# Feed-forward down weights: sums by accumulating DMA a round ahead, and a re-ordered VectorE queue

## What is computed

```python
def conv_ffn(h, w_up, conv_w, conv_b, w_down):      # h = rmsnorm(x)
    u = h @ w_up                                    # 512 x 5632
    gate, up = u[..., :D_FF], u[..., D_FF:]         # D_FF = 2816
    gp = jnp.pad(gate, ((0, 0), (CONV_W - 1, 0), (0, 0)))
    conv = conv_b + conv_w[0] * gp[:, 0:S]
    for i in range(1, CONV_W):
        conv = conv + conv_w[i] * gp[:, i:i + S]
    return (jax.nn.silu(conv) * up) @ w_down        # x = x + this
```

## Time and profile before

| | us |
|---|---|
| median of 3 runs | 1114.54 |
| lowest and highest | 1112.5, 1115.76 |
| profiled execution: time | 1112.34 |
| profiled execution: span | 1110.5 |
| PE busy | 1078.2 |
| DVE busy | 765.6 |
| ACT busy | 490.3 |
| POOL busy | 158.5 |

### The profile page before, as it was taken

The page is one execution under the profiler, slowest core; times in us unless marked ns, Lnnn a source line. Parts: engine busy times, 40 slices in busy tenths (PEclk is TensorE's granted clock), DMA queues, the critical chain, the costliest instruction groups (busy, mean ns, idle before and its releaser), DMA issues.

```text
span 1110.5 us, 15662 instructions
## 1 busy us (share of the span) xinstructions
PE 1078.2 (97%) x5896; PEld 919.9 (83%) x5896; DVE 765.6 (69%) x1061; ACT 490.3 (44%) x755; POOL 158.5 (14%) x126
## 2 busy tenths in 40 slices
PE   6999999999999999989999999999999999999986
PEld 5888778888999888879788888878888999888886
DVE  4588666676986565998343656866676986565986
ACT  6366554443433334445652245444443433434442
POOL 6100030112000112012020221030112000112012
PEclk9999999999999999999999999999999999999998
DMA  6512032225242224241222211132225242224232
GB/s 193 157 59 74 22 112 95 94 94 169 88 146 100 95 95 154 73 141 64 76 77 95 81 52 58 59 112 95 94 94 171 86 155 92 95 94 155 72 117 88
DMA packets 39704, 112.38 MB, mean 101 GB/s; under 512 B 4769, under 2 KB 9537, under 8 KB 39650
## 3 DMA queue, kind: packets, MB, share of 16 engines
q1 hardware_dynamic: 34592, 106.45, 28.2%
q0 software_dynamic: 1152, 2.88, 1.6%
q10 hardware_dynamic: 3906, 2.31, 1.1%
HBM read 108.21 MB, written 2.88 MB: 100 GB/s over the span
## 4 chain that ended last, share of the span: by engine, by line
PE 43%; DVE 6%; ACT 2%; issue 1%; DMA 1%; POOL 0%; DVEq 0%; ACTq 0%; POOLq 0%
PE PS L444 33%; PE PS L497 6%; DVE WL L1260 1%; DVE DL_Z L1348 1%; PE PS L744 1%; ACT WH L863 1%; DVE DL_W L1348 1%; DVE X L1789 0%; PE PS L776 0%; PE PS L763 0%; DVE X L1393 0%; ACT SQ L893 0%; PE PS L747 0%; DVE DRAW_Z L1385 0%; DMA RAW<-w_down 0%
## 5 line engine op out<-in xcount | busy, mean ns | idle before, releaser
L444 PE MATMUL PS<-XH,WH 128*128 128x512 f32 x992 | 394.3, 397 | 8.7 <-DVE XL L1277 8.6
L444 PE MATMUL PS<-XH,WL 128*128 128x512 f32 x992 | 387.4, 391 | 0.0
L444 PE MATMUL PS<-XL,WH 128*128 128x512 f32 x992 | 387.1, 390 | 0.0
L444 PEld LDWEIGHTS PS<-XH,WH 128*128 128x128 f32 x992 | 186.9, 188 | 52.5 <-issue 11.4
L1260 DVE TENSOR_TENSOR WL<-WRAW,WH 128x1024 fp32r<-128x1024 f32 x137 | 193.4, 1412 | 51.5 <-ACT WH L863 50.8
L444 PEld LDWEIGHTS PS<-XL,WH 128*128 128x128 f32 x992 | 187.1, 189 | 39.2 <-issue 1.7
L444 PEld LDWEIGHTS PS<-XH,WL 128*128 128x128 f32 x992 | 186.8, 188 | 39.3
L863 ACT CAST WH<-WRAW 128x1024 fp32r<-128x1024 f32 x137 | 142.4, 1043 | 156.3 <-DMA WRAW<-w_up 99.5
L1834 POOL TENSOR_TENSOR CV<-CV,R 128x512 f32<-128x512 f32 x40 | 62.1, 1553 | 498.7 <-ACT CV L909 498.7
L497 PE MATMUL PS<-AH,DH_Z 128*128 128x256 f32 x352 | 99.5, 283 | 7.9 <-DVE X L1393 7.3
L1294 DVE TENSOR_TENSOR GS<-PS,R 128x512 f32<-128x512 f32 x44 | 30.4, 692 | 110.7 <-PE PS L444 110.5
(11 more groups left out here) (219 smaller groups left out, 1515.1 us busy)
## 6 DMA issues: line engine op xcount, KB each, us to landing
WRAW<-w_up SPq DMA_DIRECT2D x88, 512.0 KB, 3.2
WRAW<-w_bin SPq DMA_DIRECT2D x24, 512.0 KB, 3.2
DRAW_W<-w_down SPq DMA_DIRECT2D x24, 384.0 KB, 3.7
DRAW_W<-w_down SPq DMA_DIRECT2D x24, 320.0 KB, 3.4
WRAW<-w_qkv SPq DMA_DIRECT2D x11, 512.0 KB, 4.5
RAW<-w_down SPq DMA_DIRECT2D x12, 384.0 KB, 3.0
RAW<-w_down SPq DMA_DIRECT2D x12, 320.0 KB, 2.9
WRAW<-w_o SPq DMA_DIRECT2D x7, 512.0 KB, 3.2
```

Of the source, the lines that this page charges most:

```text
L444: last = mm(PS[:, bank], w[:, c:c + P], x[:, kb], start=start and n == 0 and w is wh and x is hi, stop=stop and n == len(kbs) - 1 and w is wl)
```

## The change

- The sums Z1 and Z3 of all rounds are made by DMA: SP loads W21 into one of four buffers WSUM0 to WSUM3 (which lie over RW and GS, free in the down phase), and POOL's accumulating DMA adds W22 or W11. `sum_z1` and `sum_z3` are gone from DVE. The loads for rounds n+1 and n+2 are issued at the start of the phase, those for n+3 in round n+1.
- The 40 multiplications of silu by R on POOL and 4 on DVE are gone; `values` on DVE multiplies the value half from PSUM by R into RW (44 times), and `gated` multiplies the silu onto it. PE's up units wait for `value_ready` where they waited for `gated_ready`.
- The low parts of X (`x_lo`) move from rounds n+1 to n+3 all into round n+3.
- Around the start of the down phase and in all rounds, low parts, sums and takes change places in DVE's queue; ACT's follow at the start. The zeroing of GS's first columns is done for each chunk.

The core of the diff:

```diff
-        RAW21 = place("RAW21", [P, PAIRS[0] * P], at=place_at[0] - 32 * TH)
-        RAW22 = place("RAW22", [P, PAIRS[0] * P], at=place_at[0] - 20 * TH)
+        sums_at = place_at[0] - 32 * TH
         GS = place("GS", [P, 2, T + 2])
+        WSUM = [place(f"WSUM{i}", [P, PAIRS[0] * P], at=sums_at + 4 * i * PAIRS[0] * P) for i in range(4)]
+        assert sums_at + 16 * PAIRS[0] * P <= place_at[0]
...
+        def with_sum(n, name):
+
+            if n % 4 == 0:
+                return DRAW["Z1"] if name == "Z1" else Z3RAW
+            return WSUM[((3, 1) if name == "Z1" else (0, 2))[n % 2 == 0]]
 
...
+            def load_21(n, name):
+
+                sp.dma_start(with_sum(n, name)[:, 0:down_cols(n)], quarter(n, "W21"))\
+                    .then_inc(first_half[name, n % 2], 16)
 
...
                 sp.wait_ge(unit_done, u0 + last)
                 load_down(n, "W22")
-                sp.wait_ge(t_ready, FT * layer + F0[chunk] + 2 * PAIRS[chunk])
-                load_21(n + 1)
+                sp.wait_ge(conv_ready, FT * layer + F0[chunk] + 2 * PAIRS[chunk])
+                load_21(n + 1, "Z1")
                 sp.wait_ge(al_ready, AL_LAYER * layer + AL_COUNT[chunk] + 2 * PAIRS[chunk] + 1)
-                load_22(n + 1)
+                load_21(n + 1, "Z3")
+                load_21(n + 2, "Z1")
+                load_21(n + 2, "Z3")
 
             def load_round(n, src, next_unit):
 
                 r = n % 4
-                if r in (1, 2):
+                if r == 1:
+                    sp.wait_ge(down_lo["Z1"], n + 1)
+                    load_21(n + 2, "Z1")
                     sp.wait_ge(down_lo["Z3"], n + 1)
-                    load_22(n + 1)
+                    load_21(n + 2, "Z3")
                 if r:
                     sp.wait_ge(down_done, COUNT[n - 1, "W22"])
                     load_down(n, "W22")
...
                     load_down(n + 1, "W11")
                     sp.wait_ge(down_done, COUNT[n, "W12"])
                     load_down(n + 1, "W12")
-                if r < 2:
-                    sp.wait_ge(summed["Z3"], later(n + 1))
-                    load_21(n + 2)
...
+            def values(layer, m, par):
+
+                dve.wait_ge(unit_done, UP[layer] + 2 * m + 2)
+                tt(RW[:, 3 * par:3 * par + 2], halves(PS[:, 2 * par + 1]), halves(R[:]), ALU.mult)\
+                    .then_inc(value_ready, 1)
+
             def gated(layer, m, par):
 
-                u = UP[layer] + 2 * m
-                dve.wait_ge(unit_done, u + 2)
-                dve.wait_ge(slr_ready, FT * layer + m + 1)
-                halves = lambda t: t.rearrange("p (h t) -> p h t", h=2)
-                tt(RW[:, 3 * par:3 * par + 2], halves(PS[:, 2 * par + 1]), halves(CV[:, par]), ALU.mult)                    .then_inc(gated_ready, 1)
+                dve.wait_ge(value_ready, FT * layer + m + 1)
+                dve.wait_ge(silu_ready, FT * layer + m + 1)
+                rows = RW[:, 3 * par:3 * par + 2]
+                tt(rows, rows, halves(CV[:, par]), ALU.mult).then_inc(gated_ready, 1)
                 dve.wait_ge(gated_ready, FT * layer + m + 1)
...
                 odd_step(pairs - 2)
+                sum_z2(n)
+                weight_lo(n, "Z1")
                 evacuate_gate(layer, f, 0)
                 lo_unit(u0 + 4 * pairs - 1)
                 odd_sums(layer, chunk, f - 1, kb - 1)
                 convolve(layer, f, 0)
                 odd_lo(layer, chunk, kb - 1)
-                sum_z2(n)
-                weight_lo(n, "Z1")
+                values(layer, f, 0)
                 weight_lo(n, "W11")
                 evacuate_gate(layer, f + 1, 1)
                 even_sums(layer, f)
-                sum_z4(n)
                 convolve(layer, f + 1, 1)
                 even_lo(layer, chunk, kb)
+                sum_z4(n)
                 weight_lo(n, "W12")
+                values(layer, f + 1, 1)
+                odd_sums(layer, chunk, f + 1, kb)
+                last_lo(layer, chunk, kb, 2, 4)
+                take_w11(n)
+                last_lo(layer, chunk, kb, 4, 7)
                 weight_lo(n, "Z2")
-                dve.wait_ge(silu_ready, FT * layer + f + 2)
-                tt(CV[:, 1], CV[:, 1], R[:], ALU.mult).then_inc(slr_ready, 1)
-                odd_sums(layer, chunk, f + 1, kb)
-                last_lo(layer, chunk, kb)
 
             def down_rounds(n, st, next_unit):
 
                 take_z1(n)
-                take_w11(n)
                 weight_lo(n, "Z4")
                 weight_lo(n, "Z3")
                 take_w12(n)
-                sum_z1(n + 1)
                 take_z2(n)
-                sum_z3(n + 1)
                 sum_z2(n + 1)
                 weight_lo(n + 1, "Z1")
                 take_z4(n)
+                weight_lo(n, "W22")
+                weight_lo(n + 1, "W11")
                 sum_z4(n + 1)
-                weight_lo(n + 1, "W11")
-                weight_lo(n, "W22")
                 for m in (n + 1, n + 2):
                     take_z3(m - 1)
                     weight_lo(m, "W12")
+                    weight_lo(m, "Z2")
+                    take_z1(m)
+                    weight_lo(m, "Z4")
+                    take_w22(m - 1)
                     weight_lo(m, "Z3")
-                    take_z1(m)
-                    weight_lo(m, "Z2")
-                    take_w22(m - 1)
-                    weight_lo(m, "Z4")
-                    if st is not None:
-                        x_lo(st, 2 * (m - 1 - n))
-                    sum_z1(m + 1)
                     take_w11(m)
-                    if st is not None:
-                        x_lo(st, 2 * (m - 1 - n) + 1)
                     take_w12(m)
                     weight_lo(m, "W22")
-                    sum_z3(m + 1)
                     take_z2(m)
                     sum_z2(m + 1)
...
                 weight_lo(m, "Z2")
                 take_w11(m)
                 weight_lo(m, "Z4")
+                take_w22(m - 1)
                 weight_lo(m, "W12")
-                take_w22(m - 1)
                 weight_lo(m, "Z3")
                 if st is not None:
-                    x_lo(st, 4)
+                    x_lo(st, 0)
                 take_z1(m)
                 if st is not None:
-                    x_lo(st, 5)
+                    x_lo(st, 1)
+                    x_lo(st, 2)
                 take_z2(m)
                 weight_lo(m, "W22")
+                if st is not None:
+                    x_lo(st, 3)
                 take_z4(m)
                 if next_unit is not None:
                     lo_unit(next_unit)
+                if st is not None:
+                    x_lo(st, 4)
                 take_z3(m)
+                if st is not None:
+                    x_lo(st, 5)
                 if next_unit is not None:
                     lo_unit(next_unit + 1)
...
-                def gate(m, j):
-                    pool.wait_ge(silu_ready, m + (FT * layer + 1))
-                    nc.gpsimd.tensor_tensor(CV[:, j], CV[:, j], R[:], ALU.mult).then_inc(slr_ready, 1)
-                    pool.wait_ge(slr_ready, m + (FT * layer + 1))
-
-                def add_quarter(n, name, onto, src):
-                    pool.wait_ge(plain[name], 16 * (n // 4 + 1))
+                def add_quarter(n, name):
+                    onto, src = with_sum(n, name), "W22" if name == "Z1" else "W11"
+                    pool.wait_ge(first_half[name, n % 2], 16 * (n // 2 + 1))
                     pool.dma_start(onto[:, 0:down_cols(n)], quarter(n, src), accum_op=ALU.add)\
-                        .then_inc(added[name], 16)
+                        .then_inc(added[name, n % 2], 16)
 
                 for chunk in range(2):
-                    f0, n = F0[chunk], 4 * (2 * layer + chunk)
-                    with pool.Fori(0, 2 * PAIRS[chunk] - 2, 2) as i:
-                        for j in range(2):
-                            gate(i + (f0 + j), j)
-                    add_quarter(n, "Z1", DRAW["Z1"], "W22")
-                    add_quarter(n, "Z3", Z3RAW, "W11")
-                    gate(f0 + 2 * PAIRS[chunk] - 2, 0)
+                    n = 4 * (2 * layer + chunk)
+                    for m in range(n, n + 3):
+                        add_quarter(m, "Z1")
+                        add_quarter(m, "Z3")
                     if chunk:
-                        for m in range(6):
+                        sum_square(st + 1, 0)
+                    add_quarter(n + 3, "Z1")
+                    if chunk:
+                        sum_square(st + 1, 1)
+                    add_quarter(n + 3, "Z3")
+                    if chunk:
+                        for m in range(2, 6):
                             sum_square(st + 1, m)
```

More of the change, by code:

```diff
@@ L264, in trunk @@
         t_ready, nt2_ready, gated_ready = sem("t_ready"), sem("nt2_ready"), sem("gated_ready")
[L265 to L268 removed]
+        plain = {name: sem(f"plain_{name}") for name in ("W11", "W12", "W22")}
```

(4 more changed lines are left out.)

86 lines of the change are left out of this document (34 added, 52 removed).

## The result

The changed kernel takes 1132.03 us (median of 4 runs, 1131.35 to 1133.58) beside 1113.92 us for the kernel before on the same chip (4 runs, 1112.5 to 1115.76): a ratio of 1.0164, 95% interval 1.0144 to 1.0183. It is slower by 18 us. The forecast was slower by 3.6 us, and the range ended at 1123.

The account below looks back on a forecast made before the run. PE, busy 97% of the span, was taken as the bound, with gaps only in the down phases; -9.1+7.6+3.0+1.7+0.4 = +3.6 us on 1114.54 gave 1118.1 us, range 1104 to 1123.

Parts of the forecast that it names:

- Part 2: Down phases: W11(n+1), issued behind three loads, lands late and holds DVE at `sum_z2`, delaying PE's W22(n): +7.6 us (3.2 to 11.6).
- part 3: Round n+1: W22's load goes behind Z3's load for n+3, so PE's Z3 waits: +3.0 us (0 to 5).
- Part 1: D1 and D3: late gaps behind long `sum_z1` and x_lo go, with D1's clock loss: -9.1 us.
- Part 4: Last round of D1: six x_lo in place of two delay PE's last product and the next gate product: +1.7 us (0 to 3).
- Part 5: Start of the phase: Z2(n) also needs its own low part behind the last AL: +0.4 us (0 to 1).
- the late bound of 7.9: D0: latest forecast landing of W11(n+1), 306.3, with the burst at 298.38.
- the forecast's own part for plain loads: W11(n+1)'s landing in D0 before the 1 us taken for accumulating DMAs; landing with it was put at 305.3, burst at 298.38.
- my late end: W11(n+1): Z3's accumulation halves its load rate while both flow, by round-robin between queues; 4 us more in the sum.
- The clock: Rival: in D1 and D3 half clock follows PE's longer waits at Z1(n+1), 2x1.7 us more, 1121.5 us; chance 0.10 for both.
- Part 6: Up phases: 44 added `values` passes of 0.69 us cost nothing under DVE's waiting; without that cover some 25 us.
- W11 in time: Rival: W11(n+1) lands as fast as DVE asks, W22(n) starts earlier, part 2 becomes -6.1: 1104.4 us, chance 0.25.

Follow-up runs that it names:

- The direct measurement: Kernel before with four unneeded 0.69 us multiplications on VectorE ahead of the low part of Z1(n+1) in each down phase: 1126.7 us, 1.0109.
- the experiment: For Part 4: changed kernel with x_lo two per round as before, 1132.31 us. For Part 6: kernel before with `values` multiplication by R alone moved, 1115.91 us.
- the one with the loads in order: Changed kernel with the two orders, W11 and W12 loaded before AL's wait, DVE's start order nearly restored, POOL's second sum earlier: 1111.38 us; without additions 1104.51.
- the two orders: Changed kernel with W21's loads for n+2 behind W11, W12 (1127.56 us); with those for n+3 behind W22, W11, W12 (1123.28); both together 1114.94.

## Why the prediction was wrong

Three steps failed. Part 2 had the landing of W11(n+1) too early in D0 and D2 (11.4 us for 7.6), part 3 had the landing of W22(n+1) as if no additions ran beside it (7.5 us for 3.0), and the half clock stood at nothing (some 5.5 us that belong to no other part). With parts 1, 4 and 5 as measured, -9.0+11.4+7.5+1.4+1.7+5.5 is 18.5 of the 20.2 us between the two spans. Nearly all of the waits, with their places and releasers, were as predicted.

**Part 1, stalls that go: right.** The late starts at Z2(n+1) and Z2(n+2) are gone, 7.0 us, and D1's half clock of the earlier trace rows with them, about 2: 9 us for the 9.1 of the sum. One count in it is off: the 16 steps of a round, 9 of 0.74 and 7 of 0.33, are 9.0 us and not 8.2, which still fits into the 11.9.

**Part 2, W11(n+1) late: right in mechanism and place, in size in D1 and D3 alone.** The wait was predicted for `sum_z2(n+1)` with DRAW_W as releaser, and it is there. The landing in D1 was put 11.8 us behind the phase's start and came at 11.9. The accumulations' share was put at 1 us (0 to 2.1) and measured 0.8 to 1.65. The late starts at Z1(n+1) and W22(n) grew by 7.9 us in all, where 7.6 was the term, but that they agree so well is luck. In D1 and D3 PE's W22(n), the product for which the part was worked out, starts 1.9 us later behind the phase's start than before, as forecast (1.8). In D0 and D2 it starts 4.7 and 4.0 us later, where the term was 2.0 (0.9 to 3.0). The half clock has only 0.9 and 0.2 us of this: DVE ends the take of Z3(n), for which that product waits, at 313.30 in D0, 19.8 us behind the phase's start, where PE had started the product at 15.9 before, and in D2 it is the same 3.8 us.

```profile
312.89 0.41 DVE L1384 TENSOR_TENSOR X<-X,PS 128x256 f32<-128x256 f32 x1
```

The late starts do not show it, since PE ran Z1(n+1) at half clock while DVE caught up. By W22(n)'s start part 2 is 11.4 us. What was mis-sized is the landing with 384 KB: W11 landed 8.8 and 8.6 us behind the burst's start in D0 and D2, and not 6.9, later than the late bound of 7.9; and without additions still 7.5 and 6.9, where the forecast's own part for plain loads was 5.9. By the Trainium skill (DMA: Bandwidth & Descriptors, SWDGE vs HWDGE vs iDMA), each DMA engine takes turns between software and hardware queues, from which I had drawn my late end. The trace does not decide it: the additions make W11 0.8 to 1.65 us later, between my two ends of 0 and 2.1.

**Part 3, W22(n+1): the term that was mis-sized.** It was +3.0 (0 to 5). The late starts at Z3(n+1) are 7.5 us: 2.50, 2.61 and 2.44 in D1, D2 and D3. The issue was right, S+4.3 for S+4.0, but the landing was taken from the earlier trace rows, 3.4 us, a row of a queue without additions. It took 4.8, and the low part began 9.9 us behind S and not 8.1. Part 2 had paid for the additions; part 3 had left them out, though one for round n+2 runs just there (POOL issues it at 486.19). Without additions that low part waited 2.67 us in D1 and not 4.07, and Z3(n+1) was 1.10 us late there and not 2.50: the forecast's 1.2. And D2 was given 0.3 us, by steps of 0.87 against products of 2.04; it lost 2.6.

**The clock: put at nothing.** It stood as a rival, for D1 and D3, at 2x1.7, and the forecast had none. The rest of the table grew by 7.1 us, 9 if D1's old half clock is counted as gone: in the down phases PE is busy for 19.1 us at half clock, where it was for 3.4, and loses half of each. Some 3.5 us of this, most of them in D0 and D2, were spent where PE would otherwise have waited for DVE, and belong to part 2. The argument was sound, a wait of 2.47 had been followed by half clock and 1.61 not; what was missed is that D0 and D2 get the longest waits, and that Z3(n+1)'s waits come in the same class. Over the down phases of all traces here, waits of 3.0 us and more were followed by half clock in every case (11 of 11), those from 2.0 to 2.9 in 10 of 17, and those under 2.0 in none. The direct measurement puts a limit to it: four waits of 3.2 us, made by 11.6 us of work, cost the median 12.4 us together with their half clock, so the clock is not simply to be added to the waits. The table's rest says where time was spent, not what would be saved without it.

**Parts 4, 5 and 6.** Part 4 was put at 1.7 us and is 1.4: late starts of 0.50 and 0.33, and 0.58 for XL; the experiment could not tell it from nothing. Part 5 was put at 0.4 us and is 1.7: the take of Z1(n), not only the low part of Z2, stands ahead of PE's Z2(n), since PE waits for a count of takes; I had read the wait by its name. Part 6, no cost, held in the experiment.

**What the sum left out** is that its terms depend on each other. The additions cost 12.6 us in the changed kernel and 6.9 in the one with the loads in order (14 and 5 by the ratios). Whether the two orders also bring more together than alone cannot be told: 4.5 and 8.8 alone and 17 together by the medians, 6 and 10 and 17 by the ratios. Rival "W11 in time" was 1104.4. With W11 alone in time the kernel ran at 1115.08, since the sum of Z1(n+1) came last then; with Z1's chain early too, at 1107.64.

**Open.** Why a plain load of 384 KB lands so late behind three others; why the clock falls behind some waits of 2.0 to 2.9 us and not behind others; and what sets one or the other pitch.

## What to carry over

A load that is moved ahead in a queue moves all the others back: for each, find the instruction that waits for it first, and put that one's load first, whatever else the buffers would allow. A sum by accumulating DMA is a chain of two transfers in place of two side by side, and its bytes cost the engines twice here; price both, and start the chain where its slack is. When the last wait of an engine is removed, look again who comes next: here W11, then the sum of Z1, then W22, each hidden within 1 or 2 us of the last.
